# Layer 0's first projection taken by halves of K, on two of four modulation sums, and the rotation angles computed on GpSimd

## The reference

```
mod = silu(c) @ w_ada[layer] + b_ada[layer]      # 6144 values: shift_m, scale_m, gate_m, shift_f, ...
h = rms_norm(x, g_mix) * (1 + scale_m) + shift_m
proj = h @ w_in[layer]                           # 1024 x 1952: latent 416, q_sb 512, k_sb 512, v_sb 512
# latent -> c_q, c_kv, k_rope;  q = rms_norm(c_q) @ w_uq;  kv = rms_norm(c_kv) @ w_ukv;  rotary with cos, sin
# two attentions, output projection: x = x + gate_m * mixed
# feed-forward (layer 0 dense, layer 1 the best 2 of 8 experts): x = x + gate_f * y
```

## Time and profile before

| what | value |
|---|---|
| median of 3 runs | 1454.08 us (1452.95 to 1455.85) |
| the profiled execution's own time | 1452.66 us |
| its span, first to last instruction | 1450.9 us |
| busy, share of the span | PE 94%, DVE 87%, ACT 65%, POOL 0% |
| mean granted TensorE clock | 0.978 |
| DMA | 467 MB, mean 322 GB/s |

### The profile page before, as it was taken

How to read it: one execution, slowest core, us unless ns; L and a number is a source line. 1 busy time by engine, 2 the same in 40 slices (tenths; PEclk the granted TensorE clock), 3 DMA queues, 4 the chain that set the end, 5 groups by cost and what they waited for, 6 DMA issues and landing times.

```text
span 1450.9 us, 18313 instructions
## 1 busy us (share of the span) xinstructions
PE 1365.2 (94%) x7090; PEld 1141.8 (79%) x7090; DVE 1263.5 (87%) x1141; ACT 942.0 (65%) x875; POOL 3.8 (0%) x35
## 2 busy tenths in 40 slices
PE   2899889999999789999999999999999999999995
PEld 2776789998987678877788887888888788888874
DVE  6878789887767879999998999998999998999997
ACT  1545443333436368877786888777778777877873
POOL 1000000000000000000000000000000000000000
PEclk9998999999899989999999999999999999999998
DMA  8973478987563149999999999999999999999992
GB/s 331 355 255 130 145 249 315 334 308 250 184 218 99 58 157 393 394 395 393 393 396 389 391 393 395 394 395 387 381 395 393 393 399 388 370 392 394 395 396 88
DMA packets 203932, 467.24 MB, mean 322 GB/s; under 512 B 8734, under 2 KB 10940, under 8 KB 203836
## 3 DMA queue, kind: packets, MB, share of 16 engines
q1 hardware_dynamic: 203836, 465.98, 86.6%
HBM read 464.90 MB, written 1.05 MB: 321 GB/s over the span
## 4 chain that ended last, share of the span: by engine, by line
PE 71%; DMA 14%; DVE 9%; ACT 4%; issue 1%; SPq 0%; DVEq 0%; ACTq 0%
PE bank L1586 15%; PE bank L1588 14%; PE bank L1587 14%; DMA raw<-in_w_ex_up 7%; DMA raw<-in_w_ex_down 5%; PE bank L1983 4%; PE bank L1984 4%; DVE w_lo L1254 3%; PE bank L2026 2%; PE bank L2028 2%; PE bank L2002 2%; ACT w_hi L568 2%; DMA raw<-in_w_ex_gate 2%; DVE ring_sum L983 1%; PE bank L1629 1%; PE bank L1607 1%
## 5 line engine op out<-in xcount | busy, mean ns | idle before, releaser
L1254 DVE TENSOR_TENSOR w_lo<-raw,w_hi 128x2048 fp32r<-128x2048 f32 x252 | 571.2, 2288 | 59.9 <-ACT w_hi L568 58.5
L568 ACT ACTIVATE w_hi<-raw 128x2048 fp32r<-128x2048 f32 x252 | 480.7, 1918 | 123.5 <-PE bank L1588 53.1
L1254 DVE TENSOR_TENSOR more_lo<-raw,more_hi 128x2048 fp32r<-128x2048 f32 x84 | 192.0, 2285 | 4.3 <-ACT more_hi L568 4.1
L544 ACT ACTIVATE w_hi<-raw 128x2048 fp32r<-128x2048 f32 (+1 forms) x54 | 102.3, 1897 | 131.4 <-PE bank L1588 118.7
L568 ACT ACTIVATE more_hi<-raw 128x2048 fp32r<-128x2048 f32 x84 | 161.3, 1921 | 36.4 <-PE bank L1588 17.5
L1586 PE MATMUL bank<-w_hi,hg_hi 128*128 128x512 f32 x336 | 136.5, 406 | 3.1 <-DVE w_lo L1254 2.6
L912 DVE TENSOR_TENSOR w_lo<-raw,w_hi 128x2048 fp32r<-128x2048 f32 (+1 forms) x54 | 121.7, 2258 | 19.6 <-ACT w_hi L544 19.4
L1983 PE MATMUL bank<-w_hi,gs_pack 128*128 128x512 f32 x336 | 135.3, 403 | 0.0
L1588 PE MATMUL bank<-w_hi,hg_lo 128*128 128x512 f32 x336 | 132.9, 396 | 0.0
L1587 PE MATMUL bank<-w_lo,hg_hi 128*128 128x512 f32 x336 | 132.9, 395 | 0.0
L1984 PE MATMUL bank<-w_lo,gs_pack 128*128 128x512 f32 x336 | 132.7, 395 | 0.0
(11 more groups left out here) (316 smaller groups left out, 2471.9 us busy)
## 6 DMA issues: line engine op xcount, KB each, us to landing
raw<-in_w_ex_gate SPq DMA_DIRECT2D x112, 1024.0 KB, 12.5
raw<-in_w_ex_up SPq DMA_DIRECT2D x112, 1024.0 KB, 13.1
raw<-in_w_ex_down SPq DMA_DIRECT2D x112, 1024.0 KB, 13.3
raw<-in_w_ada SPq DMA_DIRECT2D x48, 1024.0 KB, 6.5
raw<-in_w_in SPq DMA_DIRECT2D x12, 1024.0 KB, 7.7
raw<-in_w_ff_gate SPq DMA_DIRECT2D x10, 1024.0 KB, 6.3
raw<-in_w_ff_up SPq DMA_DIRECT2D x10, 1024.0 KB, 5.9
raw<-in_w_ff_down SPq DMA_DIRECT2D x10, 1024.0 KB, 6.6
```

Of the source, the lines that this page charges most:

```text
L544: act_e.activation(w_hi[:, s % SPLIT, 0:words], raw[:, n % RAW, 0:words], ACT.Copy).then_inc(hi_done, 1)
L568: act_e.activation(dst, raw[:, (N0 + n) % RAW, :], ACT.Copy).then_inc(hi_done, 1)
L1254: dve.tensor_tensor(lo, raw[:, (N0 + n) % RAW, :], hi.bitcast(F32), ALU.subtract).then_inc(lo_done, 1)
```

## The change

- The four chunks are loaded and summed in the order 0, 2, 1, 3, so that the first two give shift and gain for the upper half of K (columns 0 to 511 of `h`), the other two for the lower half.
- After two chunks DVE forms the first half of shift and gain (`first_mod(0, ...)`), ACT applies it to four of the eight blocks, and PE multiplies the upper halves of K of the latent, v and q (`rows_half`, `columns_half`); the sums of chunks 1 and 3 stand between these. Then the second half of `h` is formed, and the lower halves of the latent and v follow. The transposes of the lower half leave their banks unscaled first (`late_rows`), since v uses the banks, and are scaled in place in SBUF.
- The normalised rows `y` are made after two half units instead of four. The two sums of chunk 4, which stood before the latent's variance, now stand behind its scaling, on both sides of the `w_lo` of q's second half.
- The angles are computed on POOL, each step waiting for the one before (`then`), with each multiply-and-add as two instructions; `cos2` and `sin2` are formed there too. The positions are the first of the larger transfers instead of the fourth. ACT takes the sine right after silu, ahead of its squares of `x`.

```diff
-    for u in ada_units[:8]:
-        add_ada(*u)
+        if l == 0:
+            for u in ada_units[:4]:
+                add_ada(*u)
+            add_half(w_in[l], 0, LAT, 0)
+            add_half(w_in[l], LAT + 2 * SW, SW, 0)
+            for u in ada_units[4:6]:
+                add_ada(*u)
+            add_half(w_in[l], LAT, SW, 0)
+            for u in ada_units[6:8]:
+                add_ada(*u)
+            add_half(w_in[l], 0, LAT, 1)
+            end(("lat", l), "split")
+            add_half(w_in[l], LAT + 2 * SW, SW, 1)
+            end(("v", l), "split")
+            add_next_ada(2)
+            add_half(w_in[l], LAT, SW, 1)
             add_next_ada(1)
...
+            def then(ins):
+                ins.then_inc(pool_turn, 1)
+                turned[0] += 1
+                pool.wait_ge(pool_turn, turned[0])
+            pool.wait_ge(pos_in, 16)
+            then(pool.tensor_copy(pos_f[:, :], pos_i[:, :]))
+            for g in range(G):
+                then(pool.tensor_scalar(ang[:, g, :], freq[:, :], pos_f[:, g:g + 1], None, ALU.mult))
...
+            for i in range(2):
+                for j, part in enumerate(TURN):
+                    src = ang[:, :, :] if j == 0 else rest[:, i, :, :]
+                    then(pool.tensor_scalar(trig[:, 0, :, :], turns[:, i, :, :], -part, None, ALU.mult))
+                    then(pool.tensor_tensor(rest[:, i, :, :], trig[:, 0, :, :], src, ALU.add))
...
             act_e.activation(rows2[0:8, :], rows2[0:8, :], ACT.Silu).then_inc(c_silu, 1)
+            act_e.wait_ge(angles, 1)
+            act_e.activation(trig[:, :, :, :], rest[:, :, :, :], ACT.Sin).then_inc(trig_done, 1)
...
+                    act_e.wait_ge(h_tp, 4)
+                    for j in range(2, 4):
+                        act_e.activation(hf[:, 2 * j:2 * j + 2, :], bank[j][:, :].rearrange("p (k t) -> p k t", t=T),
+                                         ACT.Copy).then_inc(late_rows, 1)
                     hi(s); s += 1
+                    act_e.wait_ge(early_mod, 2)
+                    for k in range(4):
+                        act_e.activation(hf[:, k, :], bank[k // 2][:, (k % 2) * T:(k % 2 + 1) * T], ACT.Identity,
+                                         bias=scol(0)(k), scale=gcol(0)(k)).then_inc(hf_done, 1)
+                    for _ in range(3):
+                        hi(s); s += 1
+                    act_e.wait_ge(late_rows, 2)
+                    act_e.wait_ge(mod_done, 2)
+                    for k in range(4, KD):
+                        act_e.activation(hf[:, k, :], hf[:, k, :], ACT.Identity,
+                                         bias=scol(0)(k), scale=gcol(0)(k)).then_inc(hf_done, 1)
...
+                    lo(s); s += 1
+                    dve.wait_ge(crossed, 2)
+                    first_mod(0, early_mod)
+                    split_operand(m, hf, range(2))
+                    lo(s); s += 1
+                    sum_unit()
+                    sum_unit()
+                    lo(s); s += 1
+                    sum_unit()
+                    sum_unit()
+                    lo(s); s += 1
                     dve.wait_ge(crossed, 4)
-                    mod_shift(0, 0, 4, 0)
-                    mod_gain(0, 0, 4, KD)
+                    first_mod(1, mod_done)
+                    split_operand(m, hf, range(2, 4))
                     lo(s); s += 1
-                    split_operand(m, hf)
-                    lo(s); s += 1
-                    lo(s); s += 1
-                    rotation_angles()
...
+                if l == 0:
+                    sum_unit()
                 lo(s); s += 1
                 sum_unit()
+                if l == 0:
+                    sum_unit()
...
+                if l == 0:
+                    rows_half(0, LAT, 0, m)
+                    pe.wait_ge(late_rows, 2)
+                    rows_half(2, 512, 0)
+                    across(2, 6, 4)
+                    columns_half(4, 0)
+                    across(3, 6, 12)
+                    rows_half(0, LAT, 1, m)
+                    rows_half(2, 512, 1)
```

More of the change, by code:

```diff
@@ L122, in add_half @@
             stream.append((k_rows(w, half, c0, n), 4, n, "split"))
[L124 to L128, removed]
-            add_next_ada(1)
+        if l == 0:
[14 more added lines that the diff above has]
+            add_half(w_in[l], LAT, SW, 1)
+            add_next_ada(1)
+        else:
+            add_cols(("lat", l), w_in[l], 0, LAT)
+            add_cols(("v", l), w_in[l], LAT + 2 * SW, SW)
+            add_next_ada(1)
+            for half in range(2):
+                add_half(w_in[l], LAT, SW, half)
+                add_next_ada(1)
         end(("q", l), "split")
@@ L420, in _ @@
             sp.dma_start(rows1[nb + 16:nb + 32, :], g_ffn.rearrange("l (r p) -> (l r) p", p=P)).then_inc(small_in, 16)
+            with nc.allow_non_contiguous_dma(reason="256 positions, one to a partition"):
+                sp.dma_start(pos_i[:, :], positions[0].rearrange("(g p) -> p g", p=P)).then_inc(pos_in, 16)
             for n in range(2):
@@ L925, in variance, with split_operand @@
                 ins.then_inc(var_done, 1)
-            def split_operand(m, src):
-                for j in range(4):
+            def split_operand(m, src, parts=range(4)):
+                for j in parts:
                     dve.wait_ge(hf_done, 8 * m + 2 * j + 2)
@@ L1032, in _ @@
             dve.wait_ge(cols_done, 2)
-            for _ in range(4):
+            for _ in range(2):
                 sum_unit()
@@ L1061, in _ @@
                     lo(s); s += 1
-                for _ in range(2):
-                    lo(s); s += 1
-                    sum_unit()
+                    for _ in range(2):
+                        lo(s); s += 1
+                        sum_unit()
                 variance([(0, 2, QL), (2, 4, KVL)])
@@ L1651, in rows_product, with rows_half @@
                     last.then_inc(split_used, 1)
+            def rows_half(banks, cols, half, m=None):
+                wh, wl = split_unit()
+                for g in range(G):
+                    for k in range(4):
+                        kk = 4 * half + k
+                        if g == 0:
+                            operand_slices(m, kk)
+                        last = product(bank[banks + g][:, 0:cols], h_hi[:, kk, g * P:(g + 1) * P],
+                                       h_lo[:, kk, g * P:(g + 1) * P], wh[:, k, :], wl[:, k, :], kk == 0, kk == 7)
+                last.then_inc(split_used, 1)
             def columns_half(b0, half, m=None):
@@ L1707, in _ @@
                 columns_half(4, 1)
+                if l == 0:
+                    across(RM, 6)
                 uq = plain_unit()
```

76 lines of the change are left out of this document (34 added, 42 removed).

## The result

The changed kernel is slower by half a per cent: 1460.39 and 1461.03 us against a median of 1453.51 (1452.20 to 1455.85), a ratio of 1.005 (95% interval 1.0028 to 1.0072). Run again beside other kernels it took 1461.13 (1460.77 to 1463.85), ratio 1.0054 (1.0039 to 1.0068). Two of its first four executions are left out, because they were out of all proportion (1727 and 7598 us) and nothing like them came again.

What follows compares the result with a forecast made beforehand. PE was taken to bound the kernel, fed by a nearly full DVE and full transfers. Terms 0.6 and 2.1 gave 2.7 on 1452.66, so 1455.4; with 1.4 to the median 1456.7, range 1451.5 to 1462.

Steps and rivals of the forecast that it cites:

- D: The shift in the start of k's first product on PE, at 85.36 before the change; forecast 2.7 us later.
- The likeliest case: The forecast itself: the early start is handed back and one low clock follows, 2.7 us slower; chance 0.33.
- the squares of `x` behind 15.5: A sign against the forecast: ACT's squares of `x` start later than 15.5 us, with ACT waiting for POOL.
- The start is handed back at the latent's norm: DVE idles at the latent's variance and scaling, chunk 4 and k's second half come late; L1716 starts 0.6 us later.
- The angles on POOL are hidden: At 0.31 us a step POOL's 21 steps end at 12.9, sine and load at 14.5, ahead of `x`: cost 0.
- My bound of 0.62: Upper bound in us for one of POOL's dependent angle steps, twice 0.31; at it the time would be 1462.5.
- Rival 2: POOL's angles come late and delay ACT's squares: at 0.44 us a step 1458.7, at 0.62 1462.5; chance 0.15.
- No low clock at 52.2: At the latent's lower half PE comes from 20 busy us and a short wait, so no low-clock cost.
- rival 3: Low clock also at 52.2, the latent ending 2.1 us later and what follows too: 4.8 us, 1458.9; chance 0.15.
- A low clock at L1716: PE, idle from 74.1 to 79.2, starts L1716 at the 1.2 GHz level, costing 2.1 us.
- The sum: 0.6 handed back plus 2.1 for the low clock gives 2.7 us at k's first product, 1456.7 in the median.
- Everything behind k's first product is the same: All work behind k's first product is the same in both kernels, so only its start matters.

Runs made afterwards that it cites:

- sums_ahead: The changed kernel with both sums of chunk 4 ahead of the latent's variance again; 1456.70 us, ratio 1.0029 to the kernel before the change.
- sine_late: The changed kernel with ACT's sine moved behind its rounding of q's first half, a table load on either side; 1459.44 us, ratio 1.0044.
- pool_quiet: The changed kernel with DVE's first sum made to wait until POOL has computed the angles; 1463.37 us in its one execution.
- after_fill: The changed kernel with unused products on PE ahead of its three waits (20, 32 and 20 of 256 columns); 1461.70 us, ratio 1.0068.
- both: The changed kernel with the sine behind q's first-half rounding and chunk 4's sums ahead of the latent's variance; 1454.23 us, ratio 1.0009.
- both_att: The kernel of both with 16 unused products on PE in layer 0's attention, ahead of its first keep product; 1449.16 us, ratio 0.9971.
- before_att: The kernel before the change with only 16 unused products on PE in layer 0's attention, ahead of its first keep product; 1454.09 us, ratio 1.0014.

## Why the prediction was right in its direction and where it was off

I forecast 1456.7, slower by 2.7 in D; measured were D = 8.1 in the profiled execution and about 7 to 8 in the time, inside the range. The likeliest case was too small; two rivals came true on top of it. The range held because it had been drawn for either of them. One sign that I had named as wrong did show: the squares of `x` behind 15.5, with ACT waiting for POOL. Of the signs for right, the order came as said and most of the times did not: the latent's first product at 33.3, not 30, k's second half issued at 76.5, not 71.

1. *The start is handed back at the latent's norm.* Right, step by step. DVE idles 6.6 and 1.8 (forecast 3.8 and 2.0), PE 4.2 before q's second half (forecast 4.4), and `lat_t` waits behind the rounding of k's unit, which lands 5.4 after its issue. *sums_ahead* shows that the place of chunk 4 does it: moved back, it gives 6.5 of the 8.1 at k's first product.
2. *The angles on POOL are hidden.* Wrong, and the first term that failed. I took 0.31 a step from the earlier trace rows. Alone a step takes 0.38 or 0.33, beside DVE's sums 0.82 or 0.75. The angles came at 16.9, not 12.9, the squares at 18.5, not 15.3: +3.2. My bound of 0.62 held for the mean (0.52 over the 21 steps), not for the single step, and the rows for it came from a time when DVE was still. Rival 2 named what late angles do and from which point, 0.35 a step, but not why they would be late; *sine_late* shows the first and *pool_quiet* the second. I weighed the Trainium skill's figure of twice as slow for two inputs (GPSIMD Engine Reference, section 4.1, Engine selection), and that was not the point: the two-input step is the shorter one here, 0.25 busy against 0.29. I had also laid that factor on all 21 steps, though only six have two inputs, so the 1.5 was too much. The sentence of the Trainium skill that fits stands in section 8 of the same page, Key points: POOL shares its SBUF interfaces with VectorE, with contention from VectorE's instructions in a 2-port perf mode or with two SBUF inputs. DVE's `SCALAR_TENSOR_TENSOR` has two such inputs, and the rows agree, with a factor of 2.2; no run here separates the two conditions.
3. *No low clock at 52.2.* Wrong. After an idle time of 2.99 the latent's lower half ran at 0.35 a product to 60.7 and took 7.2 (55.55 to 62.75), not 4.6: +2.6, and the squares, chunk 4 and k's unit all behind it. This was rival 3. That PE had been busy for 20 us did not protect it. It is not a fixed price either: behind the same wait the low stretch was shorter in *pool_quiet*.
4. *A low clock at L1716, +2.1.* Right in kind; it measured 1.7 (6.84 against 5.16), 1.9 in the second trace of after, and next to nothing in *pool_quiet* (5.40) behind a wait of 3.01.
5. *The sum.* 0.6 + 3.2 + 2.6 + 1.7 is 8.1, as measured. All these are read from the one trace that they explain; from other runs come 3.0 for the sine (*sine_late*) and 4.2 for the two low clocks (*after_fill*).
6. *Everything behind k's first product is the same.* Only roughly. In after the shift grew by 1.3 in attention and shrank by 1.7 towards the end; in *both* 3.8 were lost behind that product. The order is the same, but the low stretches fall elsewhere, also from one execution to the next: the two traces of after end 3.5 us apart, of which 1.4 are there at k's first product. The gain in the first 90 us and in the total must be read apart.

## What to carry to other kernels

Before a start is moved forward, ask what the last engine in the row does in the hole that it leaves: here DVE stood still at a norm, and sums moved behind that norm held a slot, so the transfer that mattered most was issued 11.2 us later than with the sums ahead of it. A small chain on POOL is not free because POOL is idle: take its steps from a stretch in which DVE works with two inputs from SBUF, and keep whatever waits for it out of ACT's way. Count PE's new waits with what may come behind them at half the clock, as a chance and not as a fixed price, and follow a shift to the end of the span by a few fixed places before believing it. One trace is one execution: two of the same kernel ended 3.5 us apart here, and two kernels that were the same up to k's first product were 1.7 apart at it.

## What the runs showed of the hardware

- POOL's steps of 32 columns take 0.25 to 0.30 with DVE still (those of 64 up to 0.37) and 0.66 to 0.74 beside `SCALAR_TENSOR_TENSOR` of 128x512 f32. DVE's own instruction does not slow: seven take 5.48 either way.
- Idle times of PE of 2.5 to 4.2 us had a stretch at the lower level begin in or behind them, each time they came between 50 and 90 us in the two traces of after. But the 3.01 ahead of L1792 in *pool_quiet* had none, the 1.32 before q's second half had one in *both* and none in both_att, and in before_att one began with no idle time over 0.83 us from 96 to 107.
- So the low stretches lie elsewhere in different executions of the same instructions. That the 10 us of spread of some kernels come from this is likely; the slowest executions have no trace.
- Products that nobody uses, 20 or 32 ahead of each wait, kept the clock at 1.00 from 36 to 111 in after's order. In attention the low level began ahead of them in each of the three kernels that had them; the median fell in one (both_att against *both*) and not in another (before_att).
- The sine right behind silu needed no table load of its own ahead of it: L622 starts as soon as the angles are there, with one load of 1.28 behind it. Where the sine stands later, in *sine_late*, there is one of 1.28 on either side of it.
